# Prompt attention scores from stacked high and low parts, with keys in block order, in a hybrid decoder step

## The chip, the cores and the metric

The kernel runs on one core of one Trainium2 chip. The time is the device time of one execution in microseconds. The engines are TensorE (PE; PEld is its weight load), VectorE (DVE), ScalarE (ACT), GpSimd (POOL) and SyncE (SP), which here only issues transfers; ACT issues some too.

## The reference

One inference step of one decoder layer, for a prompt of 1024 tokens and 8 sample tokens, all in fp32, with d_model 1024. Two branches run side by side and are merged by gates, and a feed-forward block follows:

```
lru_x, lru_g, q, k, v = split(rmsnorm(x) @ w_in)
y_lru = (rg_lru(conv(lru_x)) * gelu(lru_g)) @ w_branch_lru
q, k = rmsnorm(q) * q_gain, rmsnorm(k) * k_gain          # per head of 64
for g, (window, dil) in enumerate(((128, 1), (512, 4), (2048, 16))):
    s = q_g @ k_g.T * 64**-0.5 + bias    # per residue mod dil, banded in blocks of 128
    o_g = softmax(s) @ v_g
o = combine(o_0, o_1, o_2); y_att = o @ w_branch_att
x = x + (g_lru * y_lru + g_att * y_att) @ w_o
x = x + (silu(gate) * up) @ w_ffn_out
```

There are 24 heads, 8 in each of the three groups. The normalized keys and values are outputs as well.

## The kernel before

Activations lie transposed, channels on the 128 partitions, 1032 token columns (1024 prompt, 8 sample). Every large product is computed in a split form: a weight tile and an activation tile are each held as a high part of type fp32r and a low part (the rest), and three products of 344 columns (high-high, high-low, low-high) are accumulated. One "unit" is one output tile of 128 channels: 3 chunks of columns x 8 contraction tiles x 3 products = 72. `wraw` receives the raw weights of a unit (512 KB, from SP's queue), GpSimd splits them (cast L448, subtraction L450) into `wsp`, and PE uses them (`unit`, L472). There are two slots, one for even and one for odd units; the split of the next unit in a slot waits for `unit_done` of the one before.

The stream of stages on all engines is: values (2 pairs of units), recurrent branch `lru` (8), queries and keys `qk` (12 pairs: pairs 0 to 5 are the 12 query tiles, 6 to 11 the 12 key tiles, 4 tiles to a group), three attention stages `att0` to `att2` (4 pairs each, one pair for each two heads' tile), `ylru`, `merge`, `wo` and the feed-forward block.

The recurrent stage: DVE computes conv and scan of channel tile i, multiplies with the gate into `U` (L1286), and writes the high part (L1288) and the low part (L1289) into `big2[:, 0]` and `big2[:, 1]`. `ylru` reads both.

The `qk` stage, per unit: ACT takes the unit out of PSUM (`evac`, L991), squares it, and makes the high part of the square (L996); DVE makes its low part (`square_low`, L1270); PE sums the squares over each head with a matrix of ones (`stats`, L559); ACT takes the root (`root`, L1006); DVE takes the reciprocal (L1335) and scales (L1337) into `tmp(6 + j)`; ACT's `store` writes the result to HBM (`qkv_s`). PE puts `stats` of the other slot behind two thirds of a unit.

An attention pair: SP loads the tile of values, of queries `QT` and of keys `KTT` (512 KB each) and the two bias tiles `BT`. The query and key loads wait until the pair before has added its last bias (`sa_done`), because the tiles are single. PE turns the values (L614) and then works through four steps n of two query blocks and two heads. In a step the scores (L625) are fp32 products of 64 rows: `toks` picks the 128 queries of a block and 128 or 256 keys, which in group 1 lie 4 and in group 2 8 elements apart. DVE adds the bias (L1372), takes the maximum (L1378), ACT the exponential (L1076); PE turns the probabilities (L637) and multiplies with the values (L650); DVE copies the output (L1385), ACT stores it to `o_s` (L1084 to L1090), and DVE waits for that store before it begins the next pair. Between these, PE runs `pieces` of the two projection units of the pair (L600; one piece is three products), by the marks PIECES and, in the first pair, FIRST_PIECES: they cover the latency of the softmax.

## Time and profile before

| | before |
|---|---|
| median of 3 runs | 2072.51 us (2072.47 to 2077.44) |
| profiled execution | 2071.17 us, its span 2069.4 us |
| PE busy | 2014.0 us, 97% |
| DVE busy | 905.9 us, 44% |
| POOL busy | 552.1 us, 27% |
| ACT busy | 509.3 us, 25% |
| moved | 188.45 MB, mean 91 GB/s |
| mean granted TensorE clock | 0.993 |

The page has the busy shares, the timelines show every instruction of an engine in a stretch, and the table of stretches gives each engine's busy time in a stage. A row's idle time in brackets is that of its engine before it, with what ended it. Matmul ends are modelled, so differences between starts are the safer measure. The recurrent stage runs from about 81 to 272 us, `qk` to 580 us, the attention stages begin at about 580, 750 and 906 us and end at 1041 us.

### The profile page before, as it was taken

Reading aid. Unit: us, or ns where it says so; the run is one execution under the profiler, and the core shown is the slowest. Engines: PE = TensorE matmul, PEld = TensorE weight load, DVE = VectorE, ACT = ScalarE, POOL = GpSimd, SP = SyncE. Lnnn points to the kernel's source line nnn. Section 1 sums busy time; section 2 is a strip of 40 time slices with the busy share of each in tenths; the row PEclk is TensorE's granted clock in tenths of the full one; section 3 lists DMA queues with packets and bytes.
Section 4 is the critical chain, followed back from the end, with each engine's and each line's share of the span. In section 5 each row is a group of like instructions: output and inputs, shape, how many; then the busy total and the mean of one; then the engine's idle time right before and its main releaser. Section 6 shows DMA issues by size and latency. Waiting matters only on the chain.

```text
span 2069.4 us, 32282 instructions
## 1 busy us (share of the span) xinstructions
PE 2014.0 (97%) x12884; PEld 1952.3 (94%) x12884; DVE 905.9 (44%) x919; ACT 509.3 (25%) x726; POOL 552.1 (27%) x325
## 2 busy tenths in 40 slices
PE   7999998999989999999989899999999999999999
PEld 7999997999979999999978899999999999999999
DVE  6666677777762332222266553433311233212331
ACT  5366653333333433333311111201000000000000
POOL 2323332222211111111122143323323232323322
PEclk9999999999999999999999999999999999999999
DMA  5211111222223323334286361111111111111112
GB/s 200 97 44 43 43 46 61 93 90 81 101 97 135 116 97 136 114 111 149 87 307 236 125 239 51 44 48 51 41 51 41 51 42 49 51 41 51 41 59 84
DMA packets 71595, 188.45 MB, mean 91 GB/s; under 512 B 9313, under 2 KB 28796, under 8 KB 70780
## 3 DMA queue, kind: packets, MB, share of 16 engines
q1 hardware_dynamic: 41456, 136.97, 19.5%
q10 hardware_dynamic: 30092, 50.81, 6.7%
q8 instruction: 34, 0.56, 0.1%
q14 instruction: 13, 0.11, 0.0%
HBM read 145.09 MB, written 45.81 MB: 92 GB/s over the span
## 4 chain that ended last, share of the span: by engine, by line
PE 89%; DVE 6%; ACT 1%; issue 1%; DMA 1%; POOL 0%; ACTq 0%; SPq 0%; DVEq 0%; POOLq 0%
PE ups L472 64%; PE ups L600 13%; PE ups L625 3%; PE ups L650 3%; PE aux L637 2%; DVE x L1335 1%; PE aux L538 1%; PE aux L559 1%; PE ups L486 1%; PE aux L614 0%; DVE x L1489 0%; DVE x L1259 0%; DMA x<-o_s 0%; DVE x L1280 0%; ACT x L1076 0%
## 5 line engine op out<-in xcount | busy, mean ns | idle before, releaser
L472 PE MATMUL ups<-big,wsp 128*128 128x344 f32 x9216 | 1477.3, 321 | 9.1 <-POOL wsp L450 6.6
L472 PEld LDWEIGHTS ups<-big,wsp 128*128 128x128 f32 x9216 | 1459.4, 189 | 24.0 <-issue 16.9
L448 POOL CAST wsp<-wraw 128x1024 fp32r<-128x1024 f32 (+2 forms) x160 | 167.8, 1049 | 1485.0 <-issue 724.0
L450 POOL TENSOR_TENSOR wsp<-wraw,wsp 128x1024 fp32r<-128x1024 f32 (+2 forms) x160 | 384.0, 2400 | 12.8
L600 PE MATMUL ups<-big,wsp 128*128 128x344 f32 x1728 | 291.8, 324 | 0.0
L600 PEld LDWEIGHTS ups<-big,wsp 128*128 128x128 f32 x1728 | 272.7, 189 | 5.3 <-issue 5.2
L1335 DVE RECIPROCAL x<-x 128x1024 f32<-128x1024 f32 x24 | 157.3, 6553 | 74.4 <-ACT x L1006 74.4
L1372 DVE SCALAR_TENSOR_TENSOR x<-ups,ext 128x256 f32<-128x256 f32 (+1 forms) x96 | 48.0, 542 | 235.4 <-PE aux L637 147.4
L1181 ACT ACTIVATE ext<-ext 128x1032 f32<-128x1032 f32 x22 | 23.6, 1071 | 482.5 <-DVE ext L1589 482.4
L1591 DVE TENSOR_TENSOR ext<-ups,ext 128x1032 f32<-128x1032 f32 x22 | 27.1, 1233 | 215.4 <-PE ups L472 215.4
L1605 DVE TENSOR_TENSOR x<-ups,x 128x1032 f32 x24 | 29.6, 1233 | 203.6 <-PE ups L472 203.6
L1076 ACT ACTIVATE x<-x,ext 128x128 f32<-128x128 f32 (+1 forms) x192 | 71.2, 442 | 58.8 <-DVE ext L1380 58.4
L1594 DVE TENSOR_TENSOR ext<-ext 128x1032 f32<-128x1032 f32 x22 | 71.3, 3241 | 4.8 <-DVE ext L1591 4.8
L1589 DVE TENSOR_TENSOR ext<-ups,ext 128x1032 f32<-128x1032 f32 x22 | 27.1, 1234 | 105.3 <-PE ups L472 104.9
L625 PE MATMUL ups<-ext 64*128 64x128 f32 (+1 forms) x384 | 67.1, 476 | 4.7 <-DVEq L1357 4.7
L650 PE MATMUL ups<-x 128*128 128x65 f32 x560 | 67.8, 270 | 0.0
L650 PEld LDWEIGHTS ups<-x 128*128 128x128 f32 x560 | 66.8, 192 | 0.0
L1006 ACT ACTIVATE x<-aux,epst 128x1024 f32<-128x1024 f32 x24 | 26.8, 1117 | 132.5 <-PE aux L559 122.9
L625 PEld LDWEIGHTS ups<-ext 64*128 64x128 f32 x384 | 43.5, 281 | 14.6 <-issue 13.1
L1385 DVE COPY x<-ups 128x260 f32<-128x260 f32 x48 | 20.4, 425 | 81.4 <-PE ups L650 81.4
L1066 ACT ACTIVATE x<-aux 128x768 f32<-128x768 f32 (+1 forms) x32 | 28.6, 895 | 83.6 <-PE ups L650 67.5
L1378 DVE TENSOR_REDUCE x<-x 128x2 f32<-128x256 f32 (+1 forms) x96 | 47.6, 538 | 1.6
(190 smaller groups left out, 1147.9 us busy)
## 6 DMA issues: line engine op xcount, KB each, us to landing
wraw<-w_in SPq DMA_DIRECT2D x52, 512.0 KB, 3.4
wraw<-w_ffn_in SPq DMA_DIRECT2D x44, 512.0 KB, 3.2
out_qkv<-x ACTq DMA_DIRECT2D x28, 512.0 KB, 2.7
ext<-out_qkv SPq DMA_DIRECT2D x24, 512.0 KB, 4.3
x<-x_T SPq DMA_DIRECT2D x16, 516.0 KB, 8.2
x<-gate_s SPq DMA_DIRECT2D x16, 516.0 KB, 4.1
wraw<-w_merge SPq DMA_DIRECT2D x16, 512.0 KB, 4.9
wraw<-w_ffn_out SPq DMA_DIRECT2D x16, 512.0 KB, 3.5
```

The costliest lines, as they stand in the source:

```text
L448: nc.gpsimd.tensor_copy(hi, raw).then_inc(w_hi, 1)
L450: nc.gpsimd.tensor_tensor(lo, raw, hi.bitcast(F32), ALU.subtract).then_inc(w_split[slot], 1)
L472: ins = nc.tensor.matmul(ups[:, slot, c, 0:CH], wsp[:, slot, w, k, :], src[:, a, k, c * CH:(c + 1) * CH], start=(k == 0 and w + a == 0), s ...
L600: ins = nc.tensor.matmul(ups[:, 0, c, 0:CH], wsp[:, slot, w, k, :], big1[:, a2, k, c * CH:(c + 1) * CH], start=(k == 0 and w + a2 == 0), s ...
L625: ins = nc.tensor.matmul(s_bank[:, hh, 256 * m + 256 - P * nk:256 * m + 256], toks(QT, g, b)[hr], toks(KTT, g, b, nk)[hr], start=True, sto ...
L637: ins = nc.tensor.transpose(pt_bank[:, hh, c:c + P], SB[:, hh, c:c + P], ident[:])
L650: ins = nc.tensor.matmul(o_bank[:, at:at + HD + 1], PTS[:, hh, c:c + P], VTOK[:, b + 1 - nk + k, hh, :], start=(k == 0), stop=(k == nk - 1))
L1076: ins = nc.scalar.activation(SB[:, hh, cols], SB[:, hh, cols], ACT.Exp, bias=NM[:, 2 * m + hh:2 * m + hh + 1])
L1335: step.step(nc.vector.reciprocal(rms_t, rms_t))
L1372: ins = nc.vector.scalar_tensor_tensor(SB[:, :, cols], s_bank[:, :, cols], SCALE, BT[:, :, 0:P * nk][:, :, ::-1], ALU.mult, ALU.add)
L1378: ins = nc.vector.tensor_reduce(OT[:, 2 * n + m, :, HD + 1], SB[:, :, cols], AX_X, ALU.max)
L1594: step.step(nc.vector.tensor_tensor(ext[:, 1, 0:NT], ext[:, 0, 0:NT], ext[:, 1, 0:NT], ALU.mult))
```

## The change

- After the recurrence only the product goes to memory, in fp32, to `big2[:, 0]`. Its high and low parts are made later: those of channel tiles 0 to 3 at the ends of the pairs of group 1, those of 4 to 7 in the last pair of group 2 (ACT the high part, DVE the low part). `lru_part` tells `ylru` where they lie.
- In `qk`, ACT's `store` also makes a high part of each normalized tile (`QH`) and DVE's `query_low` the low part (`QL`). Key tiles of groups 1 and 2 are written in block order (`by_group`), so that the keys of a block are contiguous. SP's `parts_store` writes both parts to a new HBM tensor `hs`, four transfers of 64 partitions and 256 KB for a tile, laid out for each head as 64 rows of high part over 64 rows of low part. SP issues them behind the weights of two pairs later.
- An attention pair loads for each head the stacked queries `QS`, the stacked keys `KS`, and the keys with the parts exchanged `KX` (two transfers of 64 partitions): 8 transfers, 3 MB. They wait for the last scores of the pair before, and those of the first pair are issued inside the `qk` stage ahead of its last weights.
- The scores of a block and a head are two fp32r products of 128 rows and always 256 key columns, `QS` with `KS` and `QS` with `KX`, accumulated.
- In `qk` the order on PE at the start (`stats(1, 0)` before the second unit of pair 1) and that on DVE and ACT changes; FIRST_PIECES puts 24 pieces ahead of the first scores instead of 16.

```diff
+        hs = dram("hs", [24, 2, P, SEQ])
...
-        QT, KTT, VT = ext[:, 2, 0:SEQ], ext[:, 3, 0:SEQ], tmp(2)[:, 0:SEQ]
+        QH, QL = ([big2[:, 1, 4 + 2 * a + j, 0:SEQ] for j in range(2)] for a in range(2))
+        QS, VT = [ext_r[:, 2 + h, 0:SEQ] for h in range(2)], tmp(2)[:, 0:SEQ]
+        KS, KX = ([big2[:, 1, 2 * a + h, 0:SEQ] for h in range(2)] for a in range(2))
+
+        def by_group(ap, g):
+
+            d = (1, 4, 8)[g]
+            return ap.rearrange("p (d m) -> p m d", d=d)
+
+        def key_window(ap, g, b):
+
+            c = (P * max(b - 1, 0), 256 * (b // 2), 256 * (b // 2))[g]
+            return ap[:, c:c + 256]
+
+        def lru_part(a, k):
+
+            return big2[:, 0, k, :] if a else big2[:, 1, (k + 4) % KT, :]
...
-        FIRST_PIECES = (16, 24, 32, 38, 42, 46, 48)
+        FIRST_PIECES = (24, 32, 36, 40, 43, 46, 48)
...
                 def query_loads(i, g):
-                    for n, t in enumerate((QT, KTT)):
-                        sp.dma_start(t, qkv_s[ds(i + (12 * n + 4 * g), 1)].rearrange("a p t -> p (a t)")).then_inc(qk_ld, 16)
+                    for h in range(2):
+                        q, k = (hs[ds(i + (12 * n + 4 * g), 1), h] for n in range(2))
+                        sp.dma_start(QS[h].bitcast(F32), q.rearrange("a p t -> p (a t)")).then_inc(qk_ld, 16)
+                        sp.dma_start(KS[h].bitcast(F32), k.rearrange("a p t -> p (a t)")).then_inc(qk_ld, 16)
+                        for a in range(2):
+                            sp.dma_start(KX[h][a * HD:(a + 1) * HD].bitcast(F32), k[:, (1 - a) * HD:(2 - a) * HD].rearrange("a p t -> p (a t)")).then_inc(qk_ld, 16)
...
+                def parts_store(i, j):
+                    sp.wait_ge(ql_done[j], i + 1)
+                    for h in range(2):
+                        for a, t in enumerate((QH[j], QL[j])):
+                            sp.dma_start(hs[ds(i * 2 + j, 1), h, a * HD:(a + 1) * HD].rearrange("a p t -> p (a t)"),
+                                         t[h * HD:(h + 1) * HD].bitcast(F32)).then_inc(hs_stored[j], 16)
...
+                if name == "qk":
+                    def next_stores(i):
+                        for slot in range(2):
+                            weights(i, slot)
+                        for j in range(2):
+                            parts_store(i - 2, j)
+
+                    with sp.Fori(2, 10) as i:
+                        next_stores(i)
+                    next_stores(10)
+                    for n in range(4):
+                        sp.wait_ge(v_stored[n], 16)
+                    sp.wait_ge(hs_stored[0], 64 * 8)
+                    query_loads(0, 0)
+                    next_stores(11)
+                    continue
...
                         value_load(i, g)
+                        sp.wait_ge(s_mm, i * 4 + 16 * g)
+                        query_loads(i, g)
                         sp.wait_ge(sa_done, i * 4 + (16 * g + 1))
-                        query_loads(i, g)
                         bias_load(i, g)
...
-                            for m in range(2):
+                            for m in ((1, 0) if g == 2 else (0, 1)):
                                 b = 2 * n + m
-                                nk = nkeys(g, b)
+                                at = 128 if nkeys(g, b) == 1 and m == 0 else 256 * m
                                 for hh in range(2):
-                                    hr = slice(hh * HD, (hh + 1) * HD)
-                                    ins = nc.tensor.matmul(s_bank[:, hh, 256 * m + 256 - P * nk:256 * m + 256], toks(QT, g, b)[hr],
-                                                           toks(KTT, g, b, nk)[hr], start=True, stop=True)
+                                    for keys in (KS[hh], KX[hh]):
+                                        ins = nc.tensor.matmul(s_bank[:, hh, at:at + 256], toks(QS[hh], g, b), key_window(keys, g, b),
+                                                               start=(keys is KS[hh]), stop=(keys is KX[hh]))
...
-            def store(i, j):
+            def store(i, j, g=0):
                 act.wait_ge(qn_done[j], i + 2)
+                act.wait_ge(hs_stored[j], i * 64 + 64)
+                nc.scalar.activation(by_group(QH[j], g), tmp(6 + j)[:, 0:SEQ].rearrange("p (m d) -> p m d", d=(1, 4, 8)[g]), ACT.Copy).then_inc(qh_done[j], 1)
...
             act.wait_ge(u_done, KT + 1)
             evac(0, 0)
+            act.wait_ge(z_done, KT + 1)
+            evac(0, 1)
             act.wait_ge(lru_done, KT)
+            root(0, 0)
...
+                        if last and n == 4:
+                            act.wait_ge(s_mm, 48)
+                            for k in range(4, KT):
+                                nc.scalar.activation(lru_part(0, k), big2_f32[:, 0, k, :], ACT.Copy).then_inc(uh_done, 1)
...
-                step.step(nc.vector.tensor_tensor(U, H, GE, ALU.mult))
+                step.step(nc.vector.tensor_tensor(big2_f32[:, 0, ds(i, 1), :], H, GE, ALU.mult))
                 dve.sem_inc(z_done, 1)
-                step.step(nc.vector.tensor_copy(big2[:, 0, ds(i, 1), :], U))
-                step.step(nc.vector.tensor_tensor(big2[:, 1, ds(i, 1), :], U, big2[:, 0, ds(i, 1), :].bitcast(F32), ALU.subtract))
...
+            def query_low(i, j, g=0):
+                dve.wait_ge(qh_done[j], i + 1)
+                nc.vector.tensor_tensor(by_group(QL[j], g), tmp(6 + j)[:, 0:SEQ].rearrange("p (m d) -> p m d", d=(1, 4, 8)[g]),
+                                        by_group(QH[j].bitcast(F32), g), ALU.subtract).then_inc(ql_done[j], 1)
+
+            square_low(0, 1)
+            normed_qk(0, 0)
+            square_low(1, 0)
+            normed_qk(0, 1)
+            query_low(0, 0)
+            def next_norms(i, g=0, h=0):
                 normed_qk(i, 0)
                 square_low(i, 1)
+                query_low(i - 1, 1, h)
                 normed_qk(i, 1)
                 square_low(i + 1, 0)
+                query_low(i, 0, g)
```

## Rows read from the trace of the kernel before

**Rows 1.** Busy time of each engine by stretch: projections, attention of group 1.

```profile
328.00:577.00 249.00, 249.00 (x1529) 245.04 (x1530) 179.94 (x60) 88.03 (x101) 68.92 (x40) 0.99 0.25 88
750.80:906.70 155.90, 155.90 (x1026) 141.90 (x1025) 41.38 (x96) 52.96 (x108) 27.36 (x16) 1.00 0.34 115
```

**Rows 2.** PE's timeline around score steps of groups 0, 1 and 2: start, length, instruction.

```profile
640.91 1.14 PE L625 MATMUL ups<-ext 64*128 64x256 f32 x8
641.98 0.88 PE L637 MATMUL aux<-ident,x 128*128 128x128 f32 x6
...
791.49 4.99 PE L600 MATMUL ups<-big,wsp 128*128 128x344 f32 x30
796.41 1.75 PE L625 MATMUL ups<-ext 64*128 64x128 f32 x8
798.09 0.87 PE L637 MATMUL aux<-ident,x 128*128 128x128 f32 x6
...
811.95 0.88 PE L637 MATMUL aux<-ident,x 128*128 128x128 f32 x6
...
813.92 3.08 PE L600 MATMUL ups<-big,wsp 128*128 128x344 f32 x18
816.83 0.84 PE L637 MATMUL aux<-ident,x 128*128 128x128 f32 x6
...
828.79 1.75 PE L625 MATMUL ups<-ext 64*128 64x128 f32 x8
...
959.54 1.32 PE L625 MATMUL ups<-ext 64*128 64x128 f32 x8
960.79 0.66 PE L637 MATMUL aux<-ident,x 128*128 128x128 f32 x4
...
975.78 1.32 PE L625 MATMUL ups<-ext 64*128 64x128 f32 x8
```

**Rows 3.** PE's timeline: a projection unit, and the value transposes of group 1.

```profile
453.67 11.49 PE L472 MATMUL ups<-big,wsp 128*128 128x344 f32 x72
465.00 1.09 PE L559 MATMUL aux<-ext_r,bones_r 128*128 128x512 f32 x4
...
788.77 1.12 PE L614 MATMUL aux<-ident,x 128*128 128x128 f32 x8
789.81 1.75 PE L625 MATMUL ups<-ext 64*128 64x128 f32 x8
```

**Rows 4.** What the DMA queues moved from 1047 to 1060 us.

```profile
DMA packets 1272, 4.93 MB, mean 379 GB/s; under 512 B 96, under 2 KB 226, under 8 KB 1143
```

**Rows 5.** Timelines of DVE, ACT and POOL within one unit of the projections.

```profile
463.00 1.22 DVE L1270 TENSOR_TENSOR ext_r<-x,ext_r 128x1024 fp32r<-128x1024 f32 x1
467.27 6.55 DVE L1335 RECIPROCAL x<-x 128x1024 f32<-128x1024 f32 x1 [3.06 <-ACT x L1006]
...
459.81 1.06 ACT L996 ACTIVATE ext_r<-x 128x1024 fp32r<-128x1024 f32 x1
...
458.89 2.40 POOL L450 TENSOR_TENSOR wsp<-wraw,wsp 128x1024 fp32r<-128x1024 f32 x1
```

**Rows 6.** PE's waits from recurrence to projections, and DVE's cast there.

```profile
316.54 1.20 PE L559 MATMUL aux<-ext_r,bones_r 128*128 128x512 f32 x4 [3.01 <-DVE ext_r L1270]
327.98 2.07 PE L559 MATMUL aux<-ext_r,bones_r 128*128 128x512 f32 x4 [6.48 <-DVE ext_r L1270]
...
300.91 2.65 DVE L1288 CAST big<-x 128x1032 fp32r<-128x1032 f32 x1
```

**Rows 7.** PE's timeline: the first scores of the attention.

```profile
597.23 1.66 PE L625 MATMUL ups<-ext 64*128 64x128 f32 x8 [4.71 <-DVEq L1357]
```

**Rows 8.** ACT's timeline: the last evacuation of the last pair.

```profile
1040.39 0.55 ACT L1043 ACTIVATE ext<-ups,bmrg 128x344 f32<-128x344 f32 x1 [4.17 <-PE ups L600]
```

**Rows 9.** Timelines of DVE and POOL where both read memory at once.

```profile
288.91 2.03 DVE L1274 TENSOR_TENSOR x<-x 128x1032 f32<-128x1032 f32 x1 [2.62 <-ACT x L947]
...
287.45 2.40 POOL L450 TENSOR_TENSOR wsp<-wraw,wsp 128x1024 fp32r<-128x1024 f32 x1
```

More of the change, by code:

```diff
@@ L411, in _ @@
                         sp.dma_start(tmp(k), A["x_T"][k]).then_inc(x_loaded[k], 16)
+                if name == "qk":
+                    def next_stores(i):
+                        for slot in range(2):
+                            weights(i, slot)
+                        for j in range(2):
+                            parts_store(i - 2, j)
[8 more added lines that the diff above has]
+                    continue
                 with sp.Fori(first, iters) as i:
@@ L471, in unit @@
                             for w, a in ((0, 0), (0, 1), (1, 0)):
-                                ins = nc.tensor.matmul(ups[:, slot, c, 0:CH], wsp[:, slot, w, k, :], src[:, a, k, c * CH:(c + 1) * CH],
+                                tile = lru_part(a, k) if src is None else src[:, a, k, :]
+                                ins = nc.tensor.matmul(ups[:, slot, c, 0:CH], wsp[:, slot, w, k, :], tile[:, c * CH:(c + 1) * CH],
                                                        start=(k == 0 and w + a == 0), stop=(k == nk - 1 and w == 1))
@@ L603, in pieces @@
                                 ins.then_inc(au_mm if c < NCH - 1 else unit_done[slot], 1)
-                    pieces(0, 8)
+                    pieces(0, 16 if first else 8)
                     if first:
                         stats(1, 11)
-                        pieces(8, marks[0])
+                        pieces(16, marks[0])
                         pe.wait_ge(ps_free[1], T0["att0"] + 1)
@@ L1322, in _ @@
             with dve.Fori(1, KT) as i:
-                step.loop(i, 14, 1)
+                step.loop(i, 12, 1)
                 gated(i - 1)
@@ L1360, in _, with pair @@
                 per = 2 if g == 1 else 1
-                with dve.Fori(0, 4) as i:
-                    dve.wait_ge(qk_ld, i * 48 + 48 * (4 * g + 1))
+                def pair(i, last=False):
+                    dve.wait_ge(qk_ld, i * 144 + 144 * (4 * g + 1))
                     dve.wait_ge(o_stored, i * (16 * per) + 16 * stores)
-                    step.loop(i, 4)
                     for n in range(6):
@@ L1386, in _ @@
                                                   o_bank[:, 0:4 * (HD + 1)].rearrange("p (m h e) -> p m h e", m=2, h=2)).then_inc(o_ev, 1)
-                step.end(4)
+                        if last and n >= 4:
+                            for k in (2 * n - 4, 2 * n - 3):
+                                dve.wait_ge(uh_done, k + 1)
+                                nc.vector.tensor_tensor(lru_part(1, k), big2_f32[:, 0, k, :], lru_part(0, k).bitcast(F32), ALU.subtract).then_inc(ul_done, 1)
+                    if g == 1:
+                        dve.wait_ge(uh_done, i + 1)
+                        own = ds(i, 1)
+                        nc.vector.tensor_tensor(big2[:, 0, own, :], big2_f32[:, 0, own, :], big2[:, 1, ds(i + 4, 1), :].bitcast(F32),
+                                                ALU.subtract).then_inc(ul_done, 1)
+                n = 3 if g == 2 else 4
+                with dve.Fori(0, n) as i:
+                    step.loop(i, 4)
+                    pair(i)
+                step.end(n)
+                if g == 2:
+                    pair(3, True)
                 stores += 4 * per
```

76 lines of the change are left out of this document (49 added, 27 removed).

## The prediction, made before the changed kernel was run

> **What bounds the kernel now.** I read the page first, whose shares of busy time put PE far ahead of all else, and then the table by stage: in the query/key projections (328 to 577 us) PE is busy for all 249.0 us, in the attention of group 1 for all 155.9 us, while DVE is busy for 180 and 41 us [rows 1]. So in both stages that the change touches a microsecond taken off PE is a microsecond of time, and one put on another engine costs nothing until PE waits for it. I then read the timelines at the places of the edits. The busy share says nothing about a short matmul, since ends are modelled; I take differences between starts.
>
> **Scores: the term that carries the sum.** Before, a step of two blocks and two heads is four fp32 products with 64 rows each, which the trace shows as 8 records. From its start to that of what follows it takes 641.98 - 640.91 = 1.07 us in group 0 (read contiguously, 256 columns everywhere), 798.09 - 796.41 = 1.68 us in group 1 (128 and 256 columns, every 4th element) and 960.79 - 959.54 = 1.25 us in group 2 (128 columns, every 8th) [rows 2]. Group 1 moves fewer columns than group 0 and takes longer: the stride costs. After, a step is 8 fp32r products of 256 columns, keys contiguous, only the stationary queries strided. The nearest row with the same type is a projection unit: 72 products of 344 columns in 465.00 - 453.67 = 11.33 us, 157.4 ns each [rows 3], at 2.4 GHz 143.3 of columns and 14 of overhead. So 256 columns make 106.7 + 14 = 121 ns and a step 0.97 us. Whether the strided stationary read allows that is to be seen in the value transposes of group 1, whose loads are strided alike: 8 in 789.81 - 788.77 = 1.04 us, 130 ns each [rows 3]. I take 0.97 us for group 0, 1.04 for group 1 and 0.99 for group 2, which no row of its own prices (between the two; its stride is twice that of group 1). Sum over the pairs: group 0, 4 x (3 x (1.07 - 0.97) - 0.11 for the first step, which now moves 256 columns for 128) = 0.8; group 1, 16 x 0.64 = 10.2; group 2, 16 x 0.26 = 4.2. Together -15.2 us. Bounds: at the 157 ns of the 344-column row a step is 1.26 us, which makes group 0 lose 3.5, group 1 gain 6.7, group 2 nothing: -3. At bare 107 ns: -21.
>
> The Trainium skill speaks against this edit: TensorEngine Tiling (Array Packing), section Overview, gives up to 2x for a contraction of 64 or less by row tiling, and stacking gives that up. The trace agrees that two heads run side by side; by that page and the four passes of true fp32 (FP8 and Floating Point Precision, TensorE Precision Notes) contiguous steps would come out even, and the gain would be that of the stride alone.
>
> **The change of array shape.** The 30 projection products ahead of a score step take 796.41 - 791.49 = 4.92 us, those 18 ahead of a transpose 816.83 - 813.92 = 2.91 us [rows 2]: 164 against 162 ns each, or 0.20 and 0.08 us above 157.4 ns. The 0.1 us more stands only before 64-row work. It goes where projection products precede the scores, 36 times: -3.6 us. Bounds: 0 (it stays) and -7 (as much again on leaving). The tiling page's Key Properties say that changing the mode drains TensorE, which would be this term.
>
> **Loads of a pair.** 8 transfers of 3.15 MB and the bias of 0.26 MB instead of 1.05 and 0.26. They are issued as the last scores of the pair before end and must land by the next pair's first. The shortest time for that is in group 2: 975.78 - 960.79 = 15.0 us; in group 1 it is 828.79 - 811.95 = 16.8 us [rows 2]; the work in between doesn't change. At 379 GB/s, what the queues moved in a busy stretch [rows 4], 3.41 MB take 9.0 us; with about 2 us to start and to land, some 11 us. Hidden, cost 0. By the Trainium skill, SBUF — State Buffer (Door 1: The DMA port swizzle) a transfer of 64 partitions moves at 196 GB/s; the four halves of 262 KB would take 5.4 us for 2.8 and the load 13.6 us, still inside, but barely. No row of before shows such a half.
>
> **Projections: copies and stores.** Each unit of 12.26 us gets an ACT copy of 1.06 us, the length of the copy in [rows 5], a DVE subtraction of 1.22 us like the one there, and four stores (1 MB) on SP. DVE is idle for 3.06 us between that subtraction and the next reciprocal [rows 5]; the new one goes there. 0 us, also if the key reorder doubled it, since it stands in the last 8 units. On SP the next weights stand behind stores that wait for DVE. From unit start to start: the low half of (i-2, slot 1) is done about 7.8 us into pair i, four stores take until 9.2 to issue, 1 MB moves in 2.8 us at 379 GB/s and the weights after it, so they land near 14 us. They were needed at 12.3 us for the split to start at once, and at 24.5 - 3.6 = 20.9 us (both units, less the split) for PE not to notice. 0 us.
> Once it fails: the first pair's loads, 3.15 MB, go out in the eleventh pair, ahead of the last weights. 1.05 + 3.15 + 0.52 MB from 8.7 us on at 379 GB/s are 12.5 us; landing at about 22.5 to 24 us against 20.9. I take +2.5, bounds 0 and +6.
>
> **From recurrence to projections.** PE waits here for DVE, 3.01 and 6.48 us [rows 6]. The cast (2.65 us) and a subtraction (some 1.2 us) after the last recurrence go, and PE's order of sums and units changes. Walking through with the durations of [rows 5, 6] and PE's order of units: the product ends at 300.8, where the cast begins now, the slot-1 evacuation on ACT 304.2, low squares 305.3, root 305.4, first reciprocal 305.5 to 312.1, norm 313.4; the sums of slot 1 stand at 309.6 and wait for nothing; ACT can evacuate the next slot 0 at 313.4, its low squares end at 317.8, PE wants them at 318.1. So both waits go. But DVE now does low squares, reciprocal, norm and a query's low part in a row: 317.8 + 7.9 + 1.2 + 7.9 + 1.2 = 336.0, and PE wants that at 330.4. 9.5 - 5.6: -3.9 us, bounds 0 and -9.5. The casts of the other seven channel tiles lie beside a busy PE: 0.
>
> **First pair of attention.** PE waits 4.71 us for DVE's last normalization [rows 7]. Now an ACT copy (1.06) and a subtraction (1.22) follow it, and the last sums come 0.9 us later, +3.3 us, while 8 more pieces (3.8 us) run ahead: -0.5. But those 8 pieces are missing behind the scores, where they cover the softmax; I count half of them as new waits, +1.9. I take +1.5, bounds -1 and +4.
>
> **Recurrent output in attention.** In group 1 an ACT copy and a DVE subtraction per pair, both engines under 40% busy: 0. In the last pair four of each. ACT idles 4.17 us at that place [rows 8] and 4 x 1.06 = 4.2 fit; DVE ends about 1.8 us after PE wants to go on, but PE waits for the combination's loads soon after: +0.5, bounds 0 and +4.
>
> **Sum.** -15.2 - 3.6 + 0 + 2.5 - 3.9 + 1.5 + 0.5 = -18.2 us. The profiled execution took 2071.17 us for a span of 2069.4, so 2053.0; the median of the runs, 2072.51, lies 1.3 above it. Forecast 2054.
>
> **Rivals.**
> A, the strided stationary read bounds the new products: each takes what a record of group 2 takes now, 1.25 / 8 = 156 ns. Group 2 then gains nothing, group 1 16 x 0.43 = 6.9, and the sum is -10.0 us: 2062. Against it stand the 130 ns of the value transposes; for it, that these have one fp32 operand of 128 rows only. 15%.
> B, late weights move GpSimd's split onto DVE's short work. The split's 2.4 us subtraction lies under the reciprocal now [rows 5]. A DVE product of two operands beside one took 2.03 us [rows 9] and not 1.22, and the low squares end just 465.00 - 464.22 = 0.8 us before PE wants the sums. If the weights land at 16 us and not 14, norm and low squares grow by 0.8 each, and PE waits 0.8 us in each of ten pairs: +8, 2062. It decides from a landing 15 us into the pair. 18%. The SBUF page of the Trainium skill named above would bring this case about: at its 196 GB/s the four stores take 5.4 us for 2.8, and the weights land at 16.6 us.
> C, slower than before: the loads of a pair do not land in time. It costs nothing up to 15.0 us and from there on 1 us for each us of excess in every pair of group 2, from 16.8 us on also of group 1. At 20 us it is 4 x 5.0 + 4 x 3.2 = 33 us: 2087. For it: three times the bytes, halves of 64 partitions, stores of outputs and gates in the same window; against it the 379 GB/s. 10%.
> D, more goes than I count: both array changes and bare columns, -28: 2045. 12%.
> The forecast's own case: 45%.
>
> **Numbers.** The range takes in D's side and A and B with the high ends of the small terms, and leaves C out: 2044 to 2067. A run can tell 0.3%, 6.2 us, from no change. Faster by more: the forecast, D, and most of A and B, 0.78. Within: the rest of A and B and small overruns, 0.12. Slower: C and mishaps in the projections, 0.10.
>
> **What would show it.** In the profile of after: score steps of 0.97, 1.04 and 0.99 us between starts; before them 157.4 ns per product and 0.1 us less; no PE wait at 313 and 321 us, one of 5 us near 330; a PE wait of 2 to 3 us for the split of the last query/key pair; first scores some 3 us later; no wait for the ext loads. The forecast is wrong if a step takes over 1.2 us, if PE waits for loads at a pair's first scores, or if the projection unit is longer than 12.26 us.

## The result, and the profile after

The changed kernel takes 2108.78 us (median of 4 runs, 2102.79 to 2114.16) against 2072.49 us for the kernel before on the same chip: ratio 1.017, 95% interval 1.0152 to 1.0188. The forecast was 2054 us, 2044 to 2067. The prediction was wrong, and in the sign: a gain was forecast and a loss came.

| | after |
|---|---|
| profiled execution | 2106.12 us, its span 2104.3 us |
| PE busy | 2028.0 us, 96% |
| DVE busy | 960.9 us, 46% |
| moved | 238.82 MB, mean 113 GB/s |

First the score steps, on PE's timeline of after (start, length, instruction), one of each group; they answer to [rows 2].

```profile
679.20 1.12 PE L679 MATMUL ups<-big,ext_r 128*128 128x256 f32 x8
680.16 1.03 PE L691 MATMUL aux<-ident,x 128*128 128x128 f32 x8
...
795.32 2.00 PE L679 MATMUL ups<-big,ext_r 128*128 128x256 f32 x8
797.16 0.82 PE L691 MATMUL aux<-ident,x 128*128 128x128 f32 x6
...
951.37 2.07 PE L679 MATMUL ups<-big,ext_r 128*128 128x256 f32 x8
953.28 0.60 PE L691 MATMUL aux<-ident,x 128*128 128x128 f32 x4
```

From start to start a step takes 0.96 us in group 0, as forecast, but 1.84 in group 1 and 1.91 in group 2 (forecast 1.04 and 0.99): 230 and 239 ns for a product instead of 120. The weight loads say which operand it is. These are the groups of PEld from 815 to 975 us (busy time, mean ns of one, idle before):

```profile
L654 PEld LDWEIGHTS ups<-big,wsp 128*128 128x128 f32 x602 | 94.6, 188 | 0.0
L679 PEld LDWEIGHTS ups<-big,ext_r 128*128 128x128 f32 x131 | 32.3, 331 | 1.0 <-DMA ext<-bt_s 1.0
...
L691 PEld LDWEIGHTS aux<-ident,x 128*128 128x128 f32 x88 | 9.8, 140 | 0.9 <-issue 0.6
L668 PEld LDWEIGHTS aux<-ident,x 128*128 128x128 f32 x32 | 4.2, 200 | 0.0
```

The load of the strided queries (L679) takes 331 ns on average, where the contiguous weights of a piece (L654) take 188. Of the transposes, the strided ones of the values (L668) have 200 and the contiguous ones of the probabilities (L691) 140. The sign of this was in the trace of before, in the same view over group 0 (640 to 749 us), group 1 (750 to 905) and group 2 (906 to 1040), for its own loads of the queries:

```profile
L625 PEld LDWEIGHTS ups<-ext 64*128 64x128 f32 x88 | 7.2, 185 | 2.7 <-issue 2.2
L625 PEld LDWEIGHTS ups<-ext 64*128 64x128 f32 x128 | 16.2, 322 | 3.0 <-issue 2.5
L625 PEld LDWEIGHTS ups<-ext 64*128 64x128 f32 x128 | 16.5, 326 | 3.0 <-issue 2.5
```

They take 185 ns where the queries are contiguous, and 322 and 326 ns at strides of 4 and 8 elements.

Then PE's waits that before has not, on the same timeline (in brackets the idle time and what ended it), and SP's queue ahead of the largest:

```profile
341.14 2.07 PE L614 MATMUL aux<-ext_r,bones_r 128*128 128x512 f32 x4 [7.52 <-DVE ext_r L1349]
569.32 9.84 PE L527 MATMUL ups<-big,wsp 128*128 128x344 f32 x48 [11.45 <-POOL wsp L504]
613.81 1.94 PE L668 MATMUL aux<-ident,x 128*128 128x128 f32 x8 [5.42 <-DMA x<-out_qkv]
618.94 2.08 PE L679 MATMUL ups<-big,ext_r 128*128 128x256 f32 x8 [3.19 <-DMA ext<-bt_s]
625.34 5.43 PE L654 MATMUL ups<-big,wsp 128*128 128x344 f32 x24 [4.32 <-ACT x L1111]
```

```profile
542.59 3.04 SPq L410 DMA_DIRECT2D hs<-big  x4
545.82 1.00 SPq L398 DMA_DIRECT2D ext_r<-hs  x1
...
552.26 1.07 SPq L350 DMA_DIRECT2D wraw<-w_in  x2
```

The eight loads of the first pair were issued from 545.82 us on and the last weights behind them at 552.26; GpSimd's cast began at 563.25, its subtraction ended at 569.2, and PE had stood still for 11.45 us. GpSimd's split of these weights took 1.93 + 3.92 us, beside two subtractions on DVE (563.07 to 566.98), where it takes 1.04 + 2.41 elsewhere; DVE in turn is slow where it meets GpSimd, as at the end of the recurrence (327.54 against the same line at 538.16):

```profile
327.35 2.39 POOL L504 TENSOR_TENSOR wsp<-wraw,wsp 128x1024 fp32r<-128x1024 f32 x1
565.26 3.92 POOL L504 TENSOR_TENSOR wsp<-wraw,wsp 128x1024 fp32r<-128x1024 f32 x1
...
327.54 3.29 DVE L1414 SCALAR_TENSOR_TENSOR x<-x,gqk 128x1024 f32<-128x1024 f32 x1
538.16 1.28 DVE L1414 SCALAR_TENSOR_TENSOR x<-x,gqk 128x1024 f32<-128x1024 f32 x1
```

The queues of after: transfer, count, size, median us from issue to landing.

```profile
wraw<-w_in SPq DMA_DIRECT2D x52, 512.0 KB, 5.2
hs<-big SPq DMA_DIRECT2D x96, 256.0 KB, 3.9
big<-hs SPq DMA_DIRECT2D x24, 512.0 KB, 7.5
big<-hs SPq DMA_DIRECT2D x48, 256.0 KB, 8.1
ext<-bt_s SPq DMA_DIRECT2D x12, 256.0 KB, 10.0
o_s<-x ACTq DMA_DIRECT2D x8, 264.0 KB, 6.5
```

The transfers that both kernels have land later: before it was 3.4 us for `wraw`, 5.1 for the bias and 3.8 for the 264 KB store of `o_s` (the same view of before). The halves of 64 partitions (256 KB) land in 8.1 us and the wholes of twice their size in 7.5, but the halves stand behind the wholes in each pair's loads; the bias, a whole one of 256 KB and last in line, takes 10.0.

For the balance I take the starts of the value transposes, one in each pair. The table gives the time from the span's start to the first of them, from each to the next, and from the last to the end of the span, in us. The kernels in the lower rows are those of the experiments.

| kernel | to the first | pair 0 | pairs of group 0 | group 1 | group 2 | rest |
|---|---|---|---|---|---|---|
| before | 591.5 | 42.7 | 38.5 38.5 38.5 | 39.0 39.0 39.0 39.0 | 34.5 34.5 34.5 | 1060.1 |
| after | 613.8 | 46.3 | 37.8 38.1 37.8 | 39.0 39.7 39.1 39.0 | 36.5 39.2 39.5 | 1058.3 |
| a1 | 611.1 | 46.6 | 39.8 37.8 38.5 | 35.4 38.5 35.4 36.0 | 34.2 39.7 34.7 | 1058.3 |
| c2 | 613.1 | 44.3 | 37.8 37.8 39.0 | 35.4 35.4 35.4 35.4 | 32.7 33.5 32.7 | 1057.7 |
| d1 | 606.7 | 46.2 | 37.8 37.8 37.8 | 35.4 35.4 35.4 35.4 | 32.7 32.7 32.7 | 1055.2 |
| d3 | 592.6 | 42.6 | 38.5 38.5 38.5 | 35.7 35.7 35.7 35.7 | 32.1 32.1 32.1 | 1059.4 |
| c5 | 592.5 | 49.6 | 37.8 37.8 37.8 | 35.4 35.4 35.4 35.4 | 32.7 34.0 32.7 | 1054.0 |
| d4 | 597.1 | 49.8 | 37.8 37.8 39.0 | 39.0 39.0 39.0 39.0 | 36.5 38.2 38.1 | 1058.7 |
| e1 | 595.6 | 46.6 | 38.5 38.5 38.5 | 35.7 35.7 35.7 35.7 | 32.1 32.1 32.1 | 1054.7 |

After against before: +22.3 ahead of the attention (1.9 of it in the first 43 us, where the kernels do not differ), +3.6 in pair 0, -1.8, +0.8 and +11.7 in the three groups, -1.8 behind: 34.8 us, but for rounding the difference of the spans (34.9). In group 2 the first pair is 2.0 us longer than before, the other two 4.7 and 5.0: PE idles 1.9 us in the second pair, for the bias load and for DVE's bias sum, and 1.1 in the third, whose mean granted clock was 0.96.

### The profile page after: what moved, and what is told of

Same layout as the page of the kernel before. It is cut to its first block, busy times and chain, and to the rows that moved or that the text cites. A ratio compares the mean times of both kernels' runs of the same rounds, so it can differ in the third digit from the quotient of the medians.

```text
span 2104.3 us, 32673 instructions
## 1 busy us (share of the span) xinstructions
PE 2028.0 (96%) x12884; PEld 1991.5 (95%) x12884; DVE 960.9 (46%) x935; ACT 547.5 (26%) x758; POOL 556.9 (26%) x325
## 2 busy tenths in 40 slices
DMA packets 86574, 238.82 MB, mean 113 GB/s; under 512 B 12001, under 2 KB 31484, under 8 KB 85756
## 4 chain that ended last, share of the span: by engine, by line
PE 83%; DVE 8%; DMA 3%; ACT 2%; issue 2%; SPq 1%; POOL 1%; ACTq 0%; DVEq 0%; POOLq 0%
PE ups L527 61%; PE ups L654 11%; PE ups L679 3%; PE ups L704 2%; DVE x L1412 2%; PE aux L691 2%; PE aux L593 1%; PE ups L541 1%; DMA o_s<-x 1%; PE aux L614 1%; DMA ext<-bt_s 1%; DMA wraw<-w_in 1%; ACT x L1141 0%; SPq L410 0%; POOL wsp L504 0%
## 5 line engine op out<-in xcount | busy, mean ns | idle before, releaser
L654 PE MATMUL ups<-big,wsp 128*128 128x344 f32 x1728 | 293.3, 326 | 4.3 <-ACT x L1111 4.3
L654 PEld LDWEIGHTS ups<-big,wsp 128*128 128x128 f32 x1728 | 275.5, 191 | 4.7 <-issue 4.6
L1715 DVE TENSOR_TENSOR x<-ups,x 128x1032 f32 x24 | 29.6, 1232 | 203.6 <-PE ups L527 203.6
L679 PE MATMUL ups<-big,ext_r 128*128 128x256 f32 x384 | 85.1, 365 | 6.0 <-DMA ext<-bt_s 5.1
L679 PEld LDWEIGHTS ups<-big,ext_r 128*128 128x128 f32 x384 | 80.9, 287 | 7.2 <-DMA ext<-bt_s 5.9
L1419 DVE TENSOR_TENSOR big<-x,big 128x1024 fp32r<-128x1024 f32 x24 | 49.8, 2079 | 2.0 <-ACT big L1056 2.0
```

What stands on the lines that cost most here:

```text
L654: ins = nc.tensor.matmul(ups[:, 0, c, 0:CH], wsp[:, slot, w, k, :], big1[:, a2, k, c * CH:(c + 1) * CH], start=(k == 0 and w + a2 == 0), s ...
L679: ins = nc.tensor.matmul(s_bank[:, hh, at:at + 256], toks(QS[hh], g, b), key_window(keys, g, b), start=(keys is KS[hh]), stop=(keys is KX[ ...
L1419: nc.vector.tensor_tensor(by_group(QL[j], g), tmp(6 + j)[:, 0:SEQ].rearrange("p (m d) -> p m d", d=(1, 4, 8)[g]), by_group(QH[j].bitcast(F ...
```

## The experiments

The theory was: (1) the strided stationary read costs the steps of groups 1 and 2, 16 x (0.80 + 0.92) = 28 us against the forecast; (2) the last weights behind the first pair's loads cost 12. The rival to (1) was that the steps are slow for another cause (the keys' windows, the output's banks) and stay so.

**a1**, queries read as they lie in the tile (other tokens than they should be in groups 1 and 2):

```diff
-toks(QS[hh], g, b), key_window(keys, g, b),
+QS[hh][:, b * P:(b + 1) * P], key_window(keys, g, b),
```

> The changed kernel, with the stationary queries of a score product read as 128 contiguous elements in every group (in groups 1 and 2 these are the wrong tokens; nothing else differs). The changed kernel took 1.84 us for a score step in group 1 and 1.91 us in group 2, but 0.96 us in group 0, where the queries are contiguous. Theory S (the strided stationary read of a 128-row fp32r product costs 110 to 120 ns each and nothing hides it): steps fall to 0.96 us in groups 1 and 2, that is 16 x 0.88 + 16 x 0.95 = 29 us less, 2080 us. Rival (the steps are long in groups 1 and 2 because of the keys' windows or the output's banks, which are the same here): steps stay at 1.84 and 1.91 us and the time at 2109 us.

Measured 2095.02 us (2087.83 to 2103.63), ratio to before 1.0119 (1.0091 to 1.0146). The steps are about 0.95 us in all groups, so it is the stationary stride. But only 14 of the 28 us came back (neither 2080 nor 2109), and the pairs became uneven. On DVE's and ACT's timelines of a1:

```profile
962.21 0.76 DVE L1466 SCALAR_TENSOR_TENSOR x<-ups,ext 128x256 f32<-128x256 f32 x2 [13.60 <-DMA o_s<-x]
...
951.02 0.61 ACTq L1164 DMA_DIRECT2D o_s<-x  x1
```

The store of the output was issued at 951.0 and DVE's first bias sum of the next pair, which waits for it, began at 962.2; PE had its first scores at 955.1 and stood waiting for ACT's exponentials behind that sum.

**a2**, the last weights ahead of the first pair's loads:

```diff
+for slot in range(2):
+    weights(11, slot)
 query_loads(0, 0)
-next_stores(11)
+for j in range(2):
+    parts_store(9, j)
```

> The changed kernel with one move on SP: the weights of the last query/key pair are issued ahead of the 3 MB of the first attention pair, not behind them. PE waited 11.4 us for those weights' split. Theory Q (a queue in order: the weights stood behind the loads): that wait goes; the loads come some 1.3 us later and still land long before the first scores, so 2109 - 11 = 2098 us. Rival (the wait only moves to the first attention pair, where PE waited 5.4, 3.2 and 4.3 us already): 2105 to 2109 us.

Measured 2096.48 us (2093.45 to 2104.09), ratio 1.0122 (1.0096 to 1.0149), 12.3 us less than after by the medians. The wait of 11.45 us is gone.

**b1 and b2**, the kernel before with only the moving keys, or only the stationary queries, read as they lie:

```diff
-toks(KTT, g, b, nk)[hr]          (b1)
+KTT[hr, (b + 1 - nk) * P:(b + 1) * P]
-toks(QT, g, b)[hr]               (b2)
+QT[hr, b * P:(b + 1) * P]
```

> The kernel before, with the moving keys of the scores read contiguously (wrong tokens in groups 1 and 2) and the stationary queries still every 4th and 8th element. It is the reading on which the forecast's score term rested. If the stride of the moving keys set the time there: a step falls from 1.68 to about 0.97 us in group 1 and from 1.25 to about 0.86 us in group 2. Theory S (it is the stationary load): a step stays at about 1.6 and 1.25 us.

> The kernel before, with the stationary queries of the scores read contiguously (wrong tokens in groups 1 and 2) and the moving keys still every 4th and 8th element. If the moving keys' stride set the time: a step stays at 1.68 us in group 1 and 1.25 us in group 2. Theory S: a step falls to about 1.0 us in group 1 and 0.86 us in group 2, the times of as many columns in group 0.

One run each: 2064.17 and 2065.48 us. PE's timelines of group 1, first b1, then b2:

```profile
807.56 1.31 PE L625 MATMUL ups<-ext 64*128 64x128 f32 x8
808.80 0.87 PE L637 MATMUL aux<-ident,x 128*128 128x128 f32 x6
```

```profile
807.92 1.61 PE L625 MATMUL ups<-ext 64*128 64x128 f32 x8
809.46 0.87 PE L637 MATMUL aux<-ident,x 128*128 128x128 f32 x6
```

A step takes 1.24 and 1.54 us instead of 1.68, in group 2 1.15 and 1.11 instead of 1.25. Neither expectation holds whole: both strides cost in the old form, each hidden in part under the other. The loads of the queries follow the stationary stride alone: 321 and 326 ns in b1, 194 and 195 in b2.

**c1 and d1** ask what delays the stores and the bias in a1. c1 leaves the loads of the shifted keys out (the cross terms of the scores are missing); d1 loads them whole, without the exchange of the halves:

```diff
-for a in range(2):
-    sp.dma_start(KX[h][a * HD:(a + 1) * HD]..., k[:, (1 - a) * HD:(2 - a) * HD]...)
+sp.dma_start(KX[h]..., k...)     (d1; in c1 nothing)
```

> The a1 kernel (after, with the stationary queries read as they lie, so scores of groups 1 and 2 are of wrong queries) with the four half-partition loads of the shifted keys left out: the second product of each score step uses the same keys again, so scores miss their cross terms. 1.05 MB less a pair on the queues, same instructions on TensorE. Theory P (the larger traffic of the change slows the store of the output, the bias and the weights, and that is what holds the pairs of a1 at 2095): landing times of the output store fall from 6.5 us toward the 3.8 us of the kernel before, VectorE's waits for it shrink, and the time falls to 2083 to 2088. Rival Q (VectorE waits for the store because of where it is issued, however little else moves): 2092 to 2096.

> The a1 kernel with the shifted keys loaded whole: two transfers of 128 partitions and 512 KB a pair instead of four of 64 partitions and 256 KB, so the same bytes. The halves are not exchanged by it, so the cross terms are wrong, as are the queries of groups 1 and 2. Without these loads (c1) the pairs reached 37.9, 35.4 and 32.7 us and the kernel 2061; with them in halves (a1) 2095. If the bytes on the queues slow the stores: 2090 to 2096. If it is the half-partition form of the transfers: 2061 to 2067. In between, 2070 to 2085, both count.

c1: 2061.32 us (2060.2 to 2064.51), ratio 0.9943 (0.9928 to 0.9958). d1: 2064.47 us (2062.98 to 2065.5), ratio 0.9957 (0.9942 to 0.9972). Both lie under before; c1 is far below both of its cases, d1 in that of the half-partition form. With the same bytes as a1, d1 is 30.5 us faster, and leaving 12.6 MB out altogether gives only 3.2 more. So it is not the bytes that cost but the form of the transfers: four of 64 partitions and 256 KB a pair in place of two of 128 and 512 KB. Whether it is the 64 partitions or the number and size, no run separates. The queues of d1:

```profile
big<-hs SPq DMA_DIRECT2D x48, 512.0 KB, 6.8
ext<-bt_s SPq DMA_DIRECT2D x12, 256.0 KB, 8.3
o_s<-x ACTq DMA_DIRECT2D x8, 264.0 KB, 3.6
```

The output store is back at 3.6 us (a1: 5.8), and from the second on all pairs of a group have one length to 0.1 us. (In the profiled executions the difference to a1 is 24.8 us: 17.3 in the pairs, 4.4 ahead of them, 3.1 behind.)

**c2**, a1 with the attention output tile doubled, so that the next pair does not wait for the store:

```diff
-dve.wait_ge(o_stored, i * (16 * per) + 16 * stores)
+OT = OTS[i % 2]
+dve.wait_ge(o_stored[i % 2], 16 * (1 + (0, 2, 6)[g] + (i // 2) * per))
```

> The a1 kernel with the attention output tile doubled: pairs write two tiles in turn, so VectorE's first bias sum of a pair no longer waits for the store of the pair before (84.7 us of its idle time in a1 between 660 and 1085 us). Scores are still of wrong queries in groups 1 and 2. Theory P (that wait has become what sets the pairs): TensorE's waits for the exponentials (11.8 us) and for the bias sum (4.0 us) go for the most part and the time falls to 2080 to 2086. Rival Q (the bias load lands as late as the store, or the exponentials wait for something else): 2092 to 2096.

(The loops over the pairs are written out for it on ACT and DVE, and a few tiles move.) Measured 2074.01 us (2072.01 to 2080.79), ratio 1.0007 (0.9996 to 1.0018): 21 us under a1, more than expected (15.8 by the profiled executions). It shows the same from the other side: the half transfers are all there, and taking away the wait for the store brings the pairs behind the first to the same lengths as d1, but for two (39.0 and 33.5 us). The 9.5 us that c2 stays above d1 lie mostly ahead of the attention.

**c3**, a2 with the first pair's value load ahead of the stores of tile 10, slot 1, and its bias load ahead of those of tile 11:

```diff
-for j in range(2):
-    parts_store(10, j)
+parts_store(10, 0)
 sp.wait_ge(qsl_done[0], 12)
 value_load(0, 0)
-parts_store(11, 0)
+parts_store(10, 1)
 ...
 bias_load(0, 0)
+parts_store(11, 0)
 parts_store(11, 1)
```

> The a2 kernel (after with the last weights of the head tiles ahead of the first pair's loads) with the first pair's value load moved ahead of the four stores of tile 10, slot 1, and its bias load ahead of the stores of tile 11, slot 0. Computes all. If the two waits of TensorE in the first pair (5.8 us for the values, 2.3 us for the bias) come from the stores that stand before those loads on SyncE's queue: 2089 to 2093. If VectorE's low part of the last tile, ahead of the first bias sum in its queue, ends last there anyway: 2094 to 2097.

Measured 2093.02 us (2091.73 to 2094.58), ratio 1.0094 (1.0079 to 1.0109). The number lies at the edge of the first case, but the trace shows the second. PE's timeline of c3:

```profile
601.16 2.04 PE L682 MATMUL ups<-big,ext_r 128*128 128x256 f32 x8 [7.19 <-DVEq L1455]
607.53 6.65 PE L657 MATMUL ups<-big,wsp 128*128 128x344 f32 x24 [4.32 <-ACT x L1114]
```

In place of 5.76 us for the values and 2.34 for the bias (a2) stands one wait of 7.19 us for DVE, which has its last normalization and the low part of the last tile to finish.

**c5**, everything that the runs pointed to: queries stored in block order too, and the edits of a2, c2 and c3. **d4** is c5 with the queries in token order again:

```diff
-next_pair(i, (i - 7) // 2)
+next_pair(i, (i - 1) % 6 // 2)          # store(): group of the query tile too
-toks(QS[hh], g, b)
+QS[hh][:, b * P:(b + 1) * P]
```

> After with everything that the runs so far point to, computing all: queries stored in block order like the keys (so that both operands of a score product are read as they lie; the loop over head tiles written out on ScalarE and VectorE for it), last weights ahead of the first pair's loads, value and bias loads of the first pair earlier, output tile doubled. Sum if the savings add: 2109 - 14 - 12 - 5 - 12 = 2066, range 2060 to 2074. Rival: strided writes of twelve more high and low parts (ScalarE 2.1 us instead of 1.0, VectorE likewise) delay the head tiles, and the savings of the pairs overlap: 2076 to 2084.

> The c5 kernel with the queries stored and read in token order again (the one part undone; last weights first, first pair's loads earlier, doubled output tile kept). Computes all. With the waits for the output store gone, the strided stationary loads should show their full price: 128 products in each of groups 1 and 2 at 231 to 238 ns instead of 119, so 4 x 4 x 0.88 + 4 x 4 x 0.95 = 29 us over c5: 2084 to 2088. If part of it is hidden under other waits, as the a1 run may suggest (14 us): 2070 to 2078.

c5: 2057.13 us (2052.56 to 2063.44), ratio 0.9926 (0.9912 to 0.9941), below the 2060 expected at best. d4: 2088.55 us (2086.58 to 2091.11), ratio 1.0068 (1.0052 to 1.0084). With the waits for the store gone, the strided stationary read shows its full price, 31.4 us (expected 29). By the undisturbed pairs it is 39.0 - 35.4 = 3.6 us in each pair of group 1 and 36.5 - 32.7 = 3.8 in each of group 2, 29.6 in eight. Its rival, that half of the price is hidden anyway, falls: what hid it in a1 was the other wait.

**d2**, c5 with a third part of each key head stored, so that the shifted keys are one whole load:

```diff
-for a, t in enumerate((QH[j], QL[j])):
+for a, t in enumerate((QH[j], QL[j], QH[j])[0:2 + keys]):
+sp.dma_start(KX[h]..., k[:, HD:P + HD]...)
```

> The c5 kernel (2057.1), with a third part of each key head stored (high, low, high again: 24 more stores of 256 KB in the head tiles), so that the shifted keys are one load of 128 partitions at an offset of 64 rows. Computes all. If half-partition loads are what costs: the first pair and the waits for weights shrink, 2050 to 2056. If the added stores, of half-partition form themselves, delay the last weights or the first pair's loads: 2057 to 2064.

Measured 2061.09 us (2058.58 to 2066.39), ratio 0.9939 (0.9924 to 0.9954), no better than c5. The pairs are even (32.7 us each in group 2), but the value transposes of the first pair start at 600.1 us instead of 592.5 and pair 0 takes 52.0: it is the expectation's second case. That the 24 more half stores in the head tiles took back what the whole loads gave is read from this; no run shows it alone.

**d3**, the kernel before with both operands read as they lie, nothing else (b1 and b2 together):

> The kernel before with both operands of its score products read as they lie (scores of groups 1 and 2 are of wrong tokens), nothing else changed. The steps of groups 1 and 2 then cost what contiguous operands give in the old, three-product form. If the strides are all that made them 1.68 and 1.25 us, steps come down to 1.07 and some 1.0, pairs to 36.5 and 33.5, time 2054 to 2059: block order would then be worth as much as the whole change. If the three-product form has a cost of its own in groups 1 and 2, as the looks at one stride at a time suggest (1.15 and 1.11 us): 2060 to 2064.

Measured 2050.8 us (2049.5 to 2051.2), ratio 0.9887 (0.9872 to 0.9902), faster than expected by either theory. (What the expectation calls the three-product form is the plain fp32 product of before.) PE's timeline of d3, groups 1 and 2:

```profile
805.61 0.93 PE L625 MATMUL ups<-ext 64*128 64x128 f32 x8
806.47 0.87 PE L637 MATMUL aux<-ident,x 128*128 128x128 f32 x6
...
958.93 0.71 PE L625 MATMUL ups<-ext 64*128 64x128 f32 x8
959.57 1.70 PE L600 MATMUL ups<-big,wsp 128*128 128x344 f32 x9
```

Steps of 0.86 and 0.64 us: read contiguously, the old form is quicker in these groups than the stacked one (0.95), which always moves 256 columns. In groups 1 and 2 nearly the whole use of the change is its block order.

**e1** makes that a kernel that computes all: ScalarE copies each normalized tile into block order once, it is stored and loaded whole (512 KB), and the scores are the old products. It also has the last weights first, the first pair's earlier loads, the doubled output tile (a2, c3, c2) and the recurrent output as in after:

```diff
+sp.dma_start(hs[ds(i * 2 + j, 1)]..., big2_f32[:, 1, 4 + j, 0:SEQ])
...
+ins = nc.tensor.matmul(s_bank[:, hh, 256 * m + 256 - P * nk:256 * m + 256], QT[hr, b * P:(b + 1) * P],
+                       KTT[hr, (b + 1 - nk) * P:(b + 1) * P], start=True, stop=True)
```

> Only the block order of the change with the old score products, computing all: the normalized query and key tiles are copied into block order by ScalarE (one copy a tile, no high and low parts, no work of VectorE for it), stored whole (512 KB, 128 partitions) and loaded whole, one query and one key transfer a pair; score products are the old unrounded ones of 64 rows, read as they lie; last weights first, doubled output tile, recurrent output as in after. Theory H (half-partition transfers slow what stands behind them, stacking is worth nothing in groups 1 and 2): weights of the head tiles land in 3.4 to 4 us again instead of 5.3, pairs of 38, 35.7 and 32.1 us, time 2043 to 2054, below c5's 2057. Rival K (any added transfer does it, or ScalarE's strided copies of 2.1 us delay the head tiles): weights land at 5 us or more, time 2055 to 2066.

Measured 2049.14 us (2048.3 to 2053.7), ratio to before 0.9885 (0.9868 to 0.9901): the fastest of all that compute everything, 24 us under before and 60 under after. The queues of e1, and below them GpSimd's wait for weights from 330 to 600 us in c5 (sum, times, longest); e1, like before, has no wait there that is put down to the weights:

```profile
wraw<-w_in SPq DMA_DIRECT2D x52, 512.0 KB, 4.1
hs<-big_f SPq DMA_DIRECT2D x24, 512.0 KB, 3.0
ext<-bt_s SPq DMA_DIRECT2D x12, 256.0 KB, 3.8
```

```profile
POOL wsp L508 <- DMA wraw<-w_in: 151.0, 10, 21.7
```

## Why the prediction was wrong, step by step

- **Scores, forecast -15.2.** This is the step that failed, and its own sign of being wrong, a step over 1.2 us, came. It put the slowness of group 1 in [rows 2] down to the moving keys and took the stationary read of the queries from the value transposes of [rows 3]. Those do load their tile with the same stride, and took 130 ns each, but the record of their load is 200 ns (140 without the stride) and that of the queries 331: the row was near in shape and not near in price. The loads of the queries themselves stood in the trace of before with 185 ns in group 0 and 322 and 326 in groups 1 and 2, and were not asked for. What makes the one load dearer than the other no run shows. Group 0 came as forecast (0.96 us for 0.97). Groups 1 and 2 cost 16 x (1.84 - 1.68) + 16 x (1.91 - 1.25) = +13.1 instead of -14.4. Rival A had the mechanism, at 156 ns a product; the price is 230 to 239 ns (d4 against c5: 31.4 us).
- **Row tiling.** By the Trainium skill, TensorEngine Tiling (Array Packing), section Overview, row tiling gives up to 2x for short contractions, and the prediction weighed this against the change and expected contiguous steps to come out even. Where both forms move 256 columns everywhere (group 0) they nearly do: 1.07 us row-tiled and 0.96 stacked. In groups 1 and 2 the row-tiled form moves fewer columns and takes 0.86 and 0.64 us (d3) against 0.95 (c5), so that stacking is worth 0.7 us a pair in group 0, 0.3 in group 1 and -0.6 in group 2 (table).
- **Change of array shape, forecast -3.6.** The kind was right, the size low: 30 products ahead of a score step take 820.44 - 815.72 = 4.72 us in after for 4.92 before, 0.2 us less where the forecast took 0.1. With the score term the forecast gave 0.5 us a pair in group 0; after shows 0.7 (38.5 to 37.8). On PE's timeline of after:

```profile
815.72 4.88 PE L654 MATMUL ups<-big,wsp 128*128 128x344 f32 x30
820.44 1.77 PE L679 MATMUL ups<-big,ext_r 128*128 128x256 f32 x7
```

- **Loads of a pair, forecast 0.** They did land in time in nearly all pairs, and of rival C, a wait for them at the first scores, only 0.8 and 1.1 us came, in two pairs of group 2 and for the bias at the end of the line: from the first issue of a pair's loads to that of the bias it is 4.9 us (680.49 to 685.40), and the bias takes 10.0 (median) to land, 15 us in all for the forecast's 11. But the step asked only whether the new transfers meet their own deadline, and not what they do to others. They lengthen the output store and the bias load, and DVE waits for the store ahead of nearly every pair. In after this lies mostly under the slow scores; once those go, the wait for the store is worth 21 us (c2) and the form of the loads, which also acts ahead of the attention, 30.5 (d1). The prediction had the half-partition form only in its sentence on the Trainium skill's page SBUF — State Buffer (Door 1: The DMA port swizzle), whose lower rate for 64 partitions put the load at 13.6 us, "still inside". The trace is no clean test of that rate (halves land in 8.1 us, wholes of twice the size in 7.5, but the halves stand behind them), and d1 shows the cost where that sentence did not look.
- **Last weights, forecast +2.5 (0 to +6).** The mechanism was right, the size was not: 12.3 us (a2). The sum had 12.5 us at 379 GB/s from the stores ahead of the loads to the landing of the weights. The stores went out at 542.59, the loads from 545.82, the weights at 552.26, and GpSimd could begin at 563.25: 20.7 us, in which the queues moved 5.71 MB at a mean of 276 GB/s, where the sum has 4.72 MB at 379. Then the split took 5.9 us instead of 3.5, because it met DVE's subtractions: 2.4 us of the wait are rival B's mechanism. The wait was not its whole cost either: see the clock below.
- **Stores and copies in the projections, forecast 0; rival B.** GpSimd did wait for weights, and its split fell onto DVE's short work: `query_low` took 3.42 us beside it (at 379.64 and 428.90) for 1.22 alone, 2.08 on average, and GpSimd's subtraction 3.26 for 2.41. PE lost only 0.55 us by it in these pairs. As forecast, 0; B's mechanism was there without its price here, and with one at both ends of the stage.
- **Recurrence to projections, forecast -3.9.** One wait of 7.52 us and one of 0.92 stand for the 9.49 of [rows 6]: -1.1. Right in kind; the queue of norm, low squares and norm on DVE ends 3 us later than walked through. The trace says why, though no run tests it alone: DVE's two scalings (L1414) took 2.63 and 3.29 us for 1.28, both beside a subtraction of GpSimd, which adds 3.4 us.
- **First pair, forecast +1.5 (-1 to +4).** +3.6 by the table (with a mean granted clock of 0.81 for 0.92 before), and more ahead of it: 3.8 us of the 8 pieces that moved there, and a wait of 5.42 us for the values; within the pair 3.19 for the bias. Values and bias stood behind half stores that wait for DVE. No step of the prediction asked what is queued behind those stores on SP. Behind them DVE itself ends last (c3), so most of it stays in c5.
- **Recurrent output, forecast +0.5.** The end of the last pair has the wait forecast (2.85 us, `big` from L1484), but the rest of the kernel is shorter by 1.8 us in after and by 4.7 in e1 against d3, the other way than forecast. A wait of PE for DVE at the combination, 4.55 us in before (at 1073.25) and in d3, stands in neither after nor e1; what took it away was not tested alone.

Of the 55 us between forecast and result, the strided loads (28) and the last weights (10, with 1 more for the clock) are shown by runs. The rest is read from the trace alone: about 11 in and ahead of the first pair, 3 at the recurrence's end, and 2 in the first 43 us, which are no part of the change. Some 4 us more of waits in group 2, and as much less than forecast from the last pair on, cancel.

## What to carry to other kernels

- Price a strided operand for the side on which it will stand, with the product length it will have, and ask the trace for its own loads: here they were on record at 322 ns for 185. A load that hid under a long product can double a short one. Storing in the order of the reader removed it here for one copy a tile.
- New traffic is not priced by its own deadline alone. List who else uses the queues in that window and which of them an engine waits for; and look at the shape of a transfer before its bytes: the same 12.6 MB cost 34 us in halves (a1 against c1) and 3 in wholes (d1).
- When a repair gives half of its price back, look for the wait that took its place before the price is doubted: a1 gave 14 us, and with the store's wait gone contiguous queries gave 31 (c5 against d4).

## What the runs showed of the hardware that was not expected

- A stationary fp32r load of 128 columns that lie 16 or 32 bytes apart takes 329 and 336 ns in the records for 189, and a 256-column product with it 230 to 239 ns for 120. The fp32 load of 64 rows in before takes 322 and 326 for 185; stride 8 costs hardly more than stride 4.
- In the row-tiled fp32 form the two strides do not add. Group 1: 1.68 us with both, 1.24 with the keys contiguous, 1.54 with the queries, 0.86 with both contiguous; group 2: 1.25, 1.15, 1.11 and 0.64.
- Four loads of 64 partitions a pair raised the landing of a 264 KB store that another engine issues from 3.6 to 5.8 us (d1, a1). How they do it, whether by their partitions or their number, and whether the half form of the stores alone (beside their number and bytes, which e1 changes too) is what delays the weights, stays open.
- GpSimd's subtraction and a two-operand instruction of DVE slow each other when they meet: 3.26 us for 2.41 and 3.42 for 1.22 in the projections of after.
- In the wait of 11.45 us the granted clock fell. PE stood still from 557.9 to 569.3 us; the clock was granted at 1.00 until 560, at 0.50 from 562 to 572 and at 1.00 again from 574. The stretches of after from 540 to 556, 556 to 569.3 and 569.3 to 579 us (length, busy time of PE, PEld, DVE, ACT, POOL, then the granted clock, DMA share, GB/s):

```profile
540.00:556.00 16.00, 15.45 (x95) 15.01 (x95) 14.19 (x7) 7.48 (x7) 0.00 (x0) 1.00 0.76 209
556.00:569.30 13.30, 1.87 (x12) 1.58 (x11) 10.94 (x4) 5.12 (x5) 5.96 (x3) 0.66 0.95 319
569.30:579.00 9.70, 9.69 (x49) 9.69 (x49) 0.00 (x0) 0.00 (x0) 3.24 (x2) 0.77 0.66 190
```

  At 1.00 the clock is at its level of 2.4 GHz, at 0.50 at 1.2 GHz, and at 0.66 and 0.77 it was at 1.2 GHz for part of the stretch. 48 products took 579.00 - 569.32 = 9.68 us for 48 x 157.4 ns = 7.56: the wait cost 2.1 us beyond its own length.
